# Depthwise convolution: TensorE's taps as three single-pass products, and another split of the taps

## The chip, the cores and the metric

The kernel runs on one core of a Trainium2 chip. The metric is the device time of one execution in microseconds (us). TensorE (PE) multiplies, VectorE (DVE), ScalarE (ACT) and GpSimd (POOL) work on tiles of 128 partitions, SyncE (SP) issues the loads; each engine works through its own list of instructions in order and waits on semaphores.

## The reference, cut to what matters

The whole program is eight sublayers over a sequence of 512 positions and 1024 channels: four mixers, each followed by a gated feed-forward layer. The change lies in the fourth mixer, a convolution module:

```
h = u @ w_pw1 + b_pw1
a, g = split(h, 2)                       # 1024 channels each
h = a * sigmoid(g)
y[s, ch] = sum over k in 0..30 of w[k, ch] * h[s - 30 + k, ch] + b[ch]
h = silu(layernorm(y))
out = h @ w_pw2 + b_pw2
```

The fourth line is the depthwise causal convolution: 31 taps for every channel, with zeros before the start of the sequence. All arrays are float32.

## The kernel before

Channels lie on partitions: 1024 channels are 8 chunks of 128, and a chunk's activations are one tile of 128 channels by 512 positions. Float32 matrix products elsewhere in the kernel are made from rounded parts: an operand becomes a high part (type fp32r, made by a ScalarE copy) and a low part (the operand less its high part), and TensorE adds three single-pass products, high by high, high by low and low by high. Lines 1298 to 1300 are such a group.

Weights come in slots of 256 columns. For every slot SyncE loads `w_raw`, ScalarE rounds it to `w_hi` (`round_half`, line 2031, two halves), GpSimd subtracts to `w_lo` (`low_part`, line 894, two halves), and TensorE multiplies. Both parts have two buffers, by the parity of the slot, so a slot is rounded only once the slot two before it is used. This stage has slots 0 to 7 (the first pointwise product; in the text they are numbered from the start of the stage) and 8 to 11 (the second).

The convolution of a chunk is shared by three engines. TensorE takes the first `PE_TAPS[c]` taps (`conv_taps`, line 1246): for a tap the stationary operand is a 128x128 diagonal with the tap's weight of each channel, the moving operand is `u_pad` from column k on, both plain float32, and the sum grows in a bank. ScalarE makes the diagonals (`diagonals`, line 2393) into two buffers, so those of chunk c wait until the taps of chunk c - 2 are done. GpSimd takes the last `POOL_TAPS[c]` taps (`pool_taps`, lines 909 to 916). VectorE takes the rest (`own_taps`, lines 2586 and 2588), and adds the sums of GpSimd (line 2591) and of TensorE (line 2593). Before the change:

```
PE_TAPS = [7, 7, 7, 7, 7, 9, 14, 15]
POOL_TAPS = [4, 4, 4, 4, 4, 4, 5, 5]
```

The order of work is written by hand on each engine:

- TensorE: slots 0 and 1; slot 2, taps 0; slot 3, taps 1; slot 4, taps 2; slot 5, taps 3, mean 0; slot 6, taps 4, mean 1; slot 7, taps 5, mean 2; taps 6, mean 3, taps 7, means 4 to 7. A mean (line 1255) adds a finished chunk over its channels. Then come the sums of squares (line 1277) and the second pointwise product. A slot waits for its banks, its low parts, and so on; the taps of a chunk wait for its gated input, its diagonals and its bank.
- VectorE: gate of chunks 0 and 1 (line 2598), own taps 0; gate of 2 and 3, own taps 1, own taps 2; gate of 4 and 5, own taps 3, own taps 4; gate of 6 and 7, own taps 5, 6 and 7.
- ScalarE: diagonals 0; rounding of slot 2; sigmoid of chunk 0 (line 2404), half of slot 3, sigmoid of chunk 1, other half of slot 3, diagonals 1 and 2; rounding of slot 4, sigmoids of 2 and 3 with the halves of slot 5, diagonals 3 and 4; slot 6, sigmoids of 4 and 5 with slot 7, diagonals 5 and 6; slot 8, sigmoids of 6 and 7 with slot 9, diagonals 7.
- GpSimd: low parts of slots 2 and 3, taps 0, low parts 4, taps 1, low parts 5, taps 2, low parts 6, taps 3, low parts 7, taps 4, low parts 8, taps 5, low parts 9, taps 6, taps 7, low parts 10.

The loop of ScalarE, whose order matters most:

```
for c in range(DC):
    if c % 2 == 0:
        round_slots(SLOT["cv"] + c, 1)
...
    round_half(SLOT["cv"] + 2 * (c // 2) + 1 + 2, c % 2)
    if c % 2 == 1:
        diagonals(c)
        if c + 1 < DC:
            diagonals(c + 1)
```

`round_slots(base, 1)` rounds both halves of slot base + 2.

Of the kernel before, what the change touches and what calls it, by code (L numbers as in the profile page):

```python
# [18 lines left out]
ALU = mybir.AluOpType  # L19
# [5 lines left out]
P = 128  # L25
# [14 lines left out]
HPG = MH // MG  # L40
NCONV = 24
TAPS = 31
PE_TAPS = [7, 7, 7, 7, 7, 9, 14, 15]
POOL_TAPS = [4, 4, 4, 4, 4, 4, 5, 5]
BIG = 1.0e30
SCORE_MASKED = -3.0e38
# [95 lines left out]
def build(nc, t, out, sublayers=8):  # L142

    with ExitStack() as ctx:
# [152 lines left out]
        ln_hi = in_big("ln_hi", [P, DC, S], 40, F32R)  # L297
        ln_lo = in_big("ln_lo", [P, DC, S], 56, F32R)
        tap_part = [in_big(f"tap_part{j}", [P, S], (17, 36)[j]) for j in range(2)]
        tap_diag = [in_big(f"tap_diag{j}", [P, 15, P], 72 + 7.5 * j) for j in range(2)]  # L300


        bank = [ctx.enter_context(nc.psum_tensor(f"bank{j}", [P, S], F32)) for j in range(8)]
# [67 lines left out]
        dve_chain = sem("dve_chain")  # L371
        y_squares = sem("y_squares")
        y_root = sem("y_root")
        sink_step = sem("sink_step")
        dt_step = sem("dt_step")
        dt_cm_in = sem("dt_cm_in")
        dt_turned = sem("dt_turned")
# [59 lines left out]
        diag_ready = sem("diag_ready")  # L437
        pe_taps_done = sem("pe_taps_done")
        taps_done = sem("taps_done")
        pool_taps_done = sem("pool_taps_done")  # L440
        own_tap_in = sem("own_tap_in")
        skip_done = sem("skip_done")
# [372 lines left out]
        def _(pool):  # L815
# [80 lines left out]

            taps_in = [0]

            def pool_taps(c):

                tap = lambda k: cols[:, ROWS["dw_w"] + DC * k + c:ROWS["dw_w"] + DC * k + c + 1]
                acc = sq[c % 2]
                k0 = TAPS - POOL_TAPS[c]
                pool.wait_ge(glu_done, c + 1)
                if c >= 1:
                    pool.wait_ge(pool_taps_done, c)
                if c >= 2:
                    pool.wait_ge(taps_done, c - 1)
                pool.tensor_scalar(acc[:], u_pad[:, c, k0:k0 + S], tap(k0), None, ALU.mult).then_inc(own_tap_in, 1)  # L909
                taps_in[0] += 1  # L910
                for k in range(k0 + 1, TAPS):
                    part = tap_part[k % 2]
                    pool.tensor_scalar(part[:], u_pad[:, c, k:k + S], tap(k), None, ALU.mult).then_inc(own_tap_in, 1)  # L913
                    taps_in[0] += 1
                    pool.wait_ge(own_tap_in, taps_in[0])
                    ins = pool.tensor_tensor(acc[:], acc[:], part[:], ALU.add)  # L916
                    if k < TAPS - 1:
                        ins.then_inc(own_tap_in, 1)
                        taps_in[0] += 1
                ins.then_inc(pool_taps_done, 1)  # L920
# [29 lines left out]
            while n < end_slot:  # L950
                if n == SLOT["out0"] + 2:
                    attention()
                if n == SLOT["odd"] + 6:
                    odd_units()
                    n = SLOT["out1"] + 2
                if n == SLOT["ssm"] + 3 + PROLOGUE // 2:
                    scan_pool(pool)
                    n = SLOT["ssm_out"] + 4
                if SLOT["cv"] + 4 <= n <= SLOT["cv"] + 10:
                    pool_taps(n - SLOT["cv"] - 4)  # L960
                if n == SLOT["cv"] + 10:
                    pool_taps(7)
                if n not in [SLOT[f"gu{f}"] for f in range(4)]:
                    low_part(n, n % 2, SLOT_K, widths.get(n, SLOT_W))

                    n += 1
                    continue
                with pool.Fori(0, FC // 2) as i:
                    for j in range(2):
                        low_part(i * 2 + (n + j), (n + j) % 2, SLOT_K, SLOT_W)  # L970
                n += N_GU
                with pool.Fori(0, 2) as i:
                    for j in range(6):
                        low_part(i * 6 + (n + j), (n + j) % 2, 8 if j % 3 < 2 else FC - 16, SLOT_W)
                n += N_DOWN
# [261 lines left out]
        def cv_pe(pe, take, freed, slot_cm, h_chunk, out_project, follows):  # L1237
            n0 = SLOT["cv"]

            def conv_taps(c):  # L1240

                pe.wait_ge(glu_done, c + 1)
                pe.wait_ge(diag_ready, c + 1)
                take(6 + c % 2, taps_done, c + 1)
                for k in range(PE_TAPS[c]):
                    ins = pe.matmul(bank[6 + c % 2][:], tap_diag[c % 2][:, k, :], u_pad[:, c, k:k + S],
                                    start=k == 0, stop=k == PE_TAPS[c] - 1)
                ins.then_inc(pe_taps_done, 1)

            def mean_part(c):  # L1250

                if c == 0:
                    take(4, centred, DC)
                pe.wait_ge(taps_done, c + 1)
                ins = pe.matmul(bank[4][:], ones[:], v_cm[:, c, :], start=c == 0, stop=c == DC - 1)  # L1255
                if c == DC - 1:
                    ins.then_inc(mean_summed, 1)

            for j in range(4):
                for q, by in enumerate((glu_done, sig_done)):  # L1260
                    dst = [take(2 * q + m, by, 2 * j + m + 1) for m in range(2)]
                    slot_cm(n0 + 2 * j + q, (n0 + 2 * j + q) % 2, lambda k: h_hi[:, k, :], lambda k: h_lo[:, k, :], dst,
                            before=h_chunk(6) if j == 0 and q == 0 else None)
                    if 2 * j + q >= 2:
                        conv_taps(2 * j + q - 2)
                    if 2 * j + q >= 5:
                        mean_part(2 * j + q - 5)
            conv_taps(6)
            mean_part(3)
            conv_taps(7)  # L1270
            for c in range(4, DC):
                mean_part(c)
            z0, r = SQ_BASE["ln"], ROOT_BASE["ln"]
            take(0, root_done, r + 1)
            for c in range(DC):
                pe.wait_ge(sq_ready, z0 + c + 1)
                pe.matmul(bank[0][:], ones[:], sq[(z0 + c) % 2][:], start=c == 0, stop=c == DC - 1).then_inc(sq_summed, 1)  # L1277
            out_project(SLOT["pw2"], 56, lambda k: ln_hi[:, k, :], lambda k: ln_lo[:, k, :],
                        before=lambda k: pe.wait_ge(h_ready, H_BASE["ln"] + k + 1), then_norm=follows(7))
# [723 lines left out]
        def _(act):  # L2003
# [382 lines left out]
            if n_sub > 6:  # L2386
                norm(6)
                def diagonals(c):
# [1 line left out]
                    if c >= 2:  # L2390
                        act.wait_ge(pe_taps_done, c - 1)
                    for k in range(PE_TAPS[c]):
                        ins = act.activation(tap_diag[c % 2][:, k, :], ident[:], ACT.Copy, scale=col("dw_w", DC * k + c))
                    ins.then_inc(diag_ready, 1)

                diagonals(0)
                for c in range(DC):

# [6 lines left out]
                                   ).then_inc(sig_done, 1)  # L2405
                    round_half(SLOT["cv"] + 2 * (c // 2) + 1 + 2, c % 2)
                    if c % 2 == 1:
                        diagonals(c)
                        if c + 1 < DC:
                            diagonals(c + 1)  # L2410
# [164 lines left out]
        def cv_dve(dve, link):  # L2575
            n0 = SLOT["cv"]
            pad = TAPS - 1
            link(dve.memset(u_pad[:, :, 0:pad], 0.0))

            def own_taps(c):  # L2580
                v = v_cm[:, c, :]
# [616 lines left out]
```

## Time and profile before

| | us |
|---|---|
| median of three runs | 2814.43 |
| lowest and highest run | 2808.67, 2814.97 |
| the profiled execution: time | 2813.69 |
| the profiled execution: span of its trace | 2811.8 |
| TensorE busy in the span | 2665.2 |
| VectorE, ScalarE, GpSimd busy in the span | 1126.8, 1069.8, 1302.6 |
| TensorE's taps (line 1246): busy, records | 64.0, 146 |
| VectorE's taps (line 2588): busy, instructions | 100.5, 133 |
| diagonals (line 2393): busy, instructions | 22.2, 73 |

The span is the time from the first to the last instruction of the trace; times inside the trace count from its start. The convolution stage lies between about 2200 and 2360. Every group of instructions has its line in the kernel, the number of instructions and the mean length of one; the idle time in square brackets is that of the engine before the instruction, with the instruction that ended it. Matmuls overlap, so their step is read from one start to the next. A float32 tap of the kernel before is one instruction in the kernel and two records in the trace.

### The profile page before, as it was taken

What the parts mean: (1) busy time and instruction counts of PE and PEld (TensorE: products, weight loads), DVE (VectorE), ACT (ScalarE), POOL (GpSimd) and SP (SyncE); (2) the same over time, 40 slices, a digit from 0 to 9 for tenths busy, and PEclk for the clock granted to TensorE, in tenths of its full rate; (3) what the DMA queues carried; (4) which work ended last, traced back from release to release, by engine and by line L of the source; (5) the groups of instructions that cost most, each with busy time, mean ns of one, the idle gap of its engine ahead of it and who ended that gap; (6) DMA issues with size and microseconds to landing.
All of it is one profiled execution on the core that took longest, in us unless ns stands there. A gap on an engine that the chain in (4) does not pass through costs nothing. (4 is left out here: it accounts for less than half of the span.)

```text
span 2811.8 us, 34699 instructions
## 1 busy us (share of the span) xinstructions
PE 2665.2 (95%) x13241; PEld 2134.3 (76%) x13241; DVE 1126.8 (40%) x1726; ACT 1069.8 (38%) x1718; POOL 1302.6 (46%) x747
## 2 busy tenths in 40 slices
PE   6997889999999899999999999999999997999998
PEld 5775558888877588888788887888888663888886
DVE  3168734222134342221237675233321497433312
ACT  3333544333236643332346555333322333433321
POOL 2322533444436534445356775444444485444441
PEclk8998889999999999999999999999999998999998
DMA  8654502323221013223221221232222210233221
GB/s 269 213 175 143 187 31 69 104 96 100 91 78 61 31 61 119 90 90 109 79 75 60 76 73 48 90 104 90 93 94 97 75 60 15 80 100 99 91 98 56
DMA packets 275967, 265.16 MB, mean 94 GB/s; under 512 B 20268, under 2 KB 274829, under 8 KB 275853
## 3 DMA queue, kind: packets, MB, share of 16 engines
q1 hardware_dynamic: 275853, 263.59, 29.5%
q8 instruction: 78, 1.28, 0.2%
q14 instruction: 36, 0.29, 0.0%
HBM read 261.47 MB, written 2.10 MB: 94 GB/s over the span
## 5 line engine op out<-in xcount | busy, mean ns | idle before, releaser
L894 POOL TENSOR_TENSOR w_lo<-w_raw,w_hi 128x1024 fp32r<-128x1024 f32 (+1 forms) x364 | 865.0, 2386 | 1272.5 <-ACT w_hi L2031 739.2
L1298 PE MATMUL bank<-h_hi,w_hi 128*128 128x512 f32 x1552 | 610.9, 394 | 16.0 <-DVE h_lo L2734 6.6
L1299 PE MATMUL bank<-h_lo,w_hi 128*128 128x512 f32 x1552 | 606.5, 391 | 0.0
L1300 PE MATMUL bank<-h_hi,w_lo 128*128 128x512 f32 x1552 | 606.3, 391 | 0.0
L2031 ACT ACTIVATE w_hi<-w_raw 128x1024 fp32r<-128x1024 f32 (+1 forms) x232 | 233.5, 1019 | 480.8 <-PE bank L1300 436.8
L1298 PEld LDWEIGHTS bank<-h_hi,w_hi 128*128 128x128 f32 x1552 | 293.2, 189 | 81.9 <-issue 16.4
L1299 PEld LDWEIGHTS bank<-h_lo,w_hi 128*128 128x128 f32 x1552 | 293.3, 189 | 62.4 <-issue 1.7
L1300 PEld LDWEIGHTS bank<-h_hi,w_lo 128*128 128x128 f32 x1552 | 293.0, 189 | 61.4
L1298 PE MATMUL bank<-a_hi,w_hi 128*128 128x512 f32 x704 | 273.9, 389 | 0.0
L1299 PE MATMUL bank<-a_lo,w_hi 128*128 128x512 f32 x704 | 273.9, 389 | 0.0
L1300 PE MATMUL bank<-a_hi,w_lo 128*128 128x512 f32 x704 | 273.9, 389 | 0.0
L2901 DVE TENSOR_TENSOR tmp<-sq,bank 128x512 f32<-128x512 f32 x88 | 60.5, 688 | 501.5 <-PE bank L1300 480.1
L2277 ACT ACTIVATE w_hi<-w_raw 128x1024 fp32r<-128x1024 f32 x176 | 182.9, 1053 | 170.1 <-PE bank L1300 167.8
L2905 DVE TENSOR_TENSOR a_lo<-tmp,a_hi 128x512 f32 x88 | 170.5, 1954 | 10.7 <-ACT a_hi L2292 10.5
L1299 PEld LDWEIGHTS bank<-a_lo,w_hi 128*128 128x128 f32 x704 | 132.2, 188 | 27.5
L1298 PEld LDWEIGHTS bank<-a_hi,w_hi 128*128 128x128 f32 x704 | 132.2, 188 | 27.5
L1300 PEld LDWEIGHTS bank<-a_hi,w_lo 128*128 128x128 f32 x704 | 132.2, 188 | 27.2
L753 POOL TENSOR_TENSOR w_lo<-w_raw,w_hi 128x1024 fp32r<-128x1024 f32 x38 | 92.3, 2434 | 96.5 <-ACT w_hi L2031 96.5
L2588 DVE SCALAR_TENSOR_TENSOR bank<-u_pad,cols,bank 128x512 f32<-128x512 f32 x125 | 94.5, 756 | 4.5
L2287 ACT ACTIVATE sq<-bank 128x512 f32<-128x512 f32 x44 | 26.3, 598 | 182.9 <-DVE tmp L2901 182.7
L2919 DVE TENSOR_TENSOR x_cm<-bank,x_cm 128x512 f32<-128x512 f32 x16 | 11.1, 692 | 197.6 <-PE bank L1300 197.6
L2921 DVE SCALAR_TENSOR_TENSOR x_cm<-bank,mod,x_cm 128x512 f32<-128x512 f32 x16 | 12.0, 751 | 195.2 <-PE bank L1300 195.2
(417 smaller groups left out, 4636.3 us busy)
## 6 DMA issues: line engine op xcount, KB each, us to landing
ada_w<-in_ada_w_dram SPq DMA_DIRECT2D x96, 512.0 KB, 6.0
w_raw<-in_ffn_gate_dram SPq DMA_DIRECT2D x22, 1024.0 KB, 5.3
w_raw<-in_ffn_up_dram SPq DMA_DIRECT2D x22, 1024.0 KB, 5.3
w_raw<-in_ffn_w_gate_dram SPq DMA_DIRECT2D x22, 1024.0 KB, 5.2
w_raw<-in_ffn_w_up_dram SPq DMA_DIRECT2D x22, 1024.0 KB, 5.2
w_raw<-in_ffn_down_dram SPq DMA_DIRECT2D x16, 1024.0 KB, 4.9
w_raw<-in_ssm_w_in_dram SPq DMA_DIRECT2D x16, 1024.0 KB, 5.2
w_raw<-in_ffn_w_down_dram SPq DMA_DIRECT2D x16, 1024.0 KB, 5.1
```

The costliest lines, as they stand in the source:

```text
L753: pool.tensor_tensor(w_lo[n % 2][:, :, half], w_raw[n % 2][:, :, half], w_hi[n % 2][:, :, half].bitcast(F32), ALU.subtract).then_inc(w_spl ...
L894: pool.tensor_tensor(w_lo[parity][:, 0:nk, half], w_raw[parity][:, 0:nk, half], w_hi[parity][:, 0:nk, half].bitcast(F32), ALU.subtract).th ...
L1298: pe.matmul(dst[m][:], hi, src_hi(k0 + k), start=first and k == 0, stop=False)
L1299: pe.matmul(dst[m][:], hi, src_lo(k0 + k), start=False, stop=False)
L1300: ins = pe.matmul(dst[m][:], lo, src_hi(k0 + k), start=False, stop=last and k == nk - 1)
L2031: act.activation(w_hi[n % 2][:, 0:nk, half], w_raw[n % 2][:, 0:nk, half], ACT.Copy).then_inc(w_rounded, 1)
L2277: act.activation(w_hi[par][:, :, half], w_raw[par][:, :, half], ACT.Copy).then_inc(w_rounded, 1)
L2287: act.activation(sq[q][:], bank[q][:], ACT.Silu).then_inc(silu_done, 1)
L2588: link(dve.scalar_tensor_tensor(out=acc[:] if k < k1 - 1 else v, in0=u_pad[:, c, k:k + S], scalar=tap(k), in1=acc[:], op0=ALU.mult, op1=AL ...
L2901: dve.tensor_tensor(tmp[q][:], sq[q][:], bank[2 + q][:], ALU.mult).then_inc(gated, 1)
L2905: dve.tensor_tensor(a_lo[:, bass.ds(i * 2 + q, 1), :], tmp[q][:].unsqueeze(1), hi, ALU.subtract).then_inc(a_ready, 1)
L2921: dve.scalar_tensor_tensor(out=x_cm[:, c, :], in0=bank[c % 4][:], scalar=mod[:, gate + c:gate + c + 1], in1=x_cm[:, c, :], op0=ALU.mult, o ...
```

## The change

TensorE's taps are made from parts as the other products are. Of the tap weights a rounded part `dw_hi` (ScalarE) and a low part `dw_lo` (VectorE) are made once, ahead of the stage. For every chunk ScalarE rounds the padded input to `u_hi` (`round_u`, 128x542), GpSimd subtracts it from the input to give `u_lo` (`split_u`, 128x542, ahead of the chunk's `pool_taps`), both in two buffers. ScalarE makes two diagonals for a tap, `diag_hi` and `diag_lo`, and TensorE three products. TensorE has 87 taps instead of 73, GpSimd the same 34, VectorE 127 instead of 141. Two semaphores carry the new order: `tap_split` (weights and rounded inputs) and `u_split` (low inputs); one unused semaphore goes.

```
-PE_TAPS = [7, 7, 7, 7, 7, 9, 14, 15]
+PE_TAPS = [9, 9, 9, 9, 9, 11, 15, 15]
...
+            def split_u(c):
+
+                pool.wait_ge(tap_split, 2 + c + 1)
+                pool.tensor_tensor(u_lo[c % 2][:], u_pad[:, c, :], u_hi[c % 2][:].bitcast(F32), ALU.subtract).then_inc(u_split, 1)
...
                 if SLOT["cv"] + 4 <= n <= SLOT["cv"] + 10:
+                    split_u(n - SLOT["cv"] - 4)
                     pool_taps(n - SLOT["cv"] - 4)
                 if n == SLOT["cv"] + 10:
+                    split_u(7)
                     pool_taps(7)
...
                 pe.wait_ge(diag_ready, c + 1)
+                pe.wait_ge(u_split, c + 1)
                 take(6 + c % 2, taps_done, c + 1)
                 for k in range(PE_TAPS[c]):
-                    ins = pe.matmul(bank[6 + c % 2][:], tap_diag[c % 2][:, k, :], u_pad[:, c, k:k + S],
-                                    start=k == 0, stop=k == PE_TAPS[c] - 1)
+                    hi, lo = diag_hi[c % 2][:, k, :], diag_lo[c % 2][:, k, :]
+                    pe.matmul(bank[6 + c % 2][:], hi, u_hi[c % 2][:, k:k + S], start=k == 0, stop=False)
+                    pe.matmul(bank[6 + c % 2][:], hi, u_lo[c % 2][:, k:k + S], start=False, stop=False)
+                    ins = pe.matmul(bank[6 + c % 2][:], lo, u_hi[c % 2][:, k:k + S], start=False, stop=k == PE_TAPS[c] - 1)
...
                     for k in range(PE_TAPS[c]):
-                        ins = act.activation(tap_diag[c % 2][:, k, :], ident[:], ACT.Copy, scale=col("dw_w", DC * k + c))
+                        at = DC * k + c
+                        act.activation(diag_hi[c % 2][:, k, :], ident[:], ACT.Copy, scale=col("dw_w", at))
+                        ins = act.activation(diag_lo[c % 2][:, k, :], ident[:], ACT.Copy, scale=dw_lo[:, at:at + 1])
                     ins.then_inc(diag_ready, 1)
 
+                def round_u(c):
+
+                    act.wait_ge(glu_done, c + 1)
+                    if c >= 2:
+                        act.wait_ge(pe_taps_done, c - 1)
+                    act.activation(u_hi[c % 2][:], u_pad[:, c, :], ACT.Copy).then_inc(tap_split, 1)
+
+                act.activation(dw_hi[:], col_range("dw_w", 0, TAPS * DC), ACT.Copy).then_inc(tap_split, 1)
+                act.wait_ge(tap_split, 2)
                 diagonals(0)
...
                     if c % 2 == 1:
+                        round_u(c - 1)
+                        round_u(c)
                         diagonals(c)
                         if c + 1 < DC:
                             diagonals(c + 1)
...
             link(dve.memset(u_pad[:, :, 0:pad], 0.0))
+            dve.wait_ge(tap_split, 1)
+            dve.tensor_tensor(dw_lo[:], col_range("dw_w", 0, TAPS * DC), dw_hi[:].bitcast(F32), ALU.subtract).then_inc(tap_split, 1)
```

## Rows read from the trace of the kernel before

**Rows 1.** Engines' busy time by stretch: PE, PEld, DVE, ACT, POOL, PEclk, DMA share, GB/s.

```profile
2210.00:2220.00 10.00, 8.39 (x37) 6.67 (x36) 3.14 (x5) 4.85 (x10) 5.08 (x3) 1.00 0.34 106
2220.00:2352.80 132.80, 132.79 (x442) 82.76 (x441) 116.81 (x155) 35.38 (x81) 112.78 (x71) 1.00 0.17 56
2352.80:2358.40 5.60, 0.00 (x0) 0.00 (x0) 4.87 (x7) 0.00 (x0) 3.98 (x3) 0.93 0.00 0
```

**Rows 2.** Chain of waits at the stage's end: start, length, what ran.

```profile
2355.61 1.27 POOL sq L916
2356.97 0.70 DVE v_cm L2591
...
2358.44 2.09 PE bank L1255 x2
```

**Rows 3.** Timeline of GpSimd in the stage: start, length, engine, line, operation.

```profile
2238.75 4.77 POOL L894 TENSOR_TENSOR w_lo<-w_raw,w_hi 128x1024 fp32r<-128x1024 f32 x2 [7.57 <-ACT w_hi L2031]
...
2309.39 4.77 POOL L894 TENSOR_TENSOR w_lo<-w_raw,w_hi 128x1024 fp32r<-128x1024 f32 x2 [6.33 <-ACT w_hi L2031]
...
2324.76 4.69 POOL L894 TENSOR_TENSOR w_lo<-w_raw,w_hi 128x1024 fp32r<-128x1024 f32 x2
2329.41 1.59 POOL L909 TENSOR_SCALAR sq<-u_pad,cols 128x512 f32<-128x512 f32 x1
...
2343.27 1.56 POOL L909 TENSOR_SCALAR sq<-u_pad,cols 128x512 f32<-128x512 f32 x1 [0.16 <-issue]
```

**Rows 4.** Timeline of ScalarE: the diagonals of chunk 6.

```profile
2304.15 4.21 ACT L2393 ACTIVATE tap_diag<-ident,cols 128x128 f32<-128x128 f32 x14 [15.05 <-PE bank L1246]
```

**Rows 5.** Timeline of VectorE: a long wait, one chunk's taps, the last tap.

```profile
2241.78 0.75 DVE L2598 SCALAR_TENSOR_TENSOR u_pad<-bank,cols,tmp 128x512 f32<-128x512 f32 x1 [5.45 <-ACT tmp L2404]
...
2285.33 14.21 DVE L2588 SCALAR_TENSOR_TENSOR bank<-u_pad,cols,bank 128x512 f32<-128x512 f32 x18
...
2355.68 0.75 DVE L2588 SCALAR_TENSOR_TENSOR v_cm<-u_pad,cols,bank 128x512 f32<-128x512 f32 x1
```

**Rows 6.** Timeline of TensorE in the stage and behind it.

```profile
2246.30 4.03 PE L1246 MATMUL bank<-u_pad,tap_diag 128*128 128x512 f32 x9
...
2262.10 0.39 PE L1299 MATMUL bank<-h_lo,w_hi 128*128 128x512 f32 x1
...
2263.00 0.39 PE L1300 MATMUL bank<-h_hi,w_lo 128*128 128x512 f32 x1
...
2280.15 6.17 PE L1246 MATMUL bank<-u_pad,tap_diag 128*128 128x512 f32 x14
2286.15 1.02 PE L1255 MATMUL bank<-v_cm,ones 128*128 128x512 f32 x2
...
2303.95 1.02 PE L1255 MATMUL bank<-v_cm,ones 128*128 128x512 f32 x2
...
2315.71 6.60 PE L1246 MATMUL bank<-u_pad,tap_diag 128*128 128x512 f32 x15
...
2350.05 2.74 PE L1255 MATMUL bank<-v_cm,ones 128*128 128x512 f32 x6
2358.44 2.08 PE L1255 MATMUL bank<-v_cm,ones 128*128 128x512 f32 x2 [5.65 <-DVE v_cm L2593]
2362.05 10.33 PE L1277 MATMUL bank<-sq,ones 128*128 128x512 f32 x16 [1.54 <-ACT sq L2416]
2379.67 0.76 PE L1298 MATMUL bank<-ln_hi,w_hi 128*128 128x512 f32 x1 [7.29 <-DVE ln_lo L3168]
...
2384.91 0.40 PE L1298 MATMUL bank<-ln_hi,w_hi 128*128 128x512 f32 x1
```

**Rows 7.** Groups by line, 2190 to 2400: busy time, mean ns of one.

```profile
L894 POOL TENSOR_TENSOR w_lo<-w_raw,w_hi 128x1024 fp32r<-128x1024 f32 x20 | 47.9, 2413 | 76.8 <-ACT w_hi L2031 76.8
...
L2423 ACT ACTIVATE ln_hi<-sq 128x512 fp32r<-128x512 f32 x4 | 2.5, 632 | 0.1
```

**Rows 8.** One tile's instructions, `tap_part`: shortest, median and longest in ns.

```profile
L916 POOL TENSOR_TENSOR sq<-sq,tap_part x26: 1259/1270/1819, 2224.1 to 2355.6; 128x512 f32<-128x512 f32 x26
```

More of the change, by code:

```diff
@@ L299, in build @@
         tap_part = [in_big(f"tap_part{j}", [P, S], (17, 36)[j]) for j in range(2)]
-        tap_diag = [in_big(f"tap_diag{j}", [P, 15, P], 72 + 7.5 * j) for j in range(2)]
+        diag_hi = [in_big(f"diag_hi{j}", [P, 15, P], 72 + 7.5 * j, F32R) for j in range(2)]
+        diag_lo = [in_big(f"diag_lo{j}", [P, 15, P], 40 + 7.5 * j, F32R) for j in range(2)]
+        u_hi = [in_big(f"u_hi{j}", [P, TAPS - 1 + S], 56 + 2.5 * j, F32R) for j in range(2)]
+        u_lo = [in_big(f"u_lo{j}", [P, TAPS - 1 + S], 61 + 2.5 * j, F32R) for j in range(2)]
+        dw_hi = in_big("dw_hi", [P, TAPS * DC], 66, F32R)
+        dw_lo = in_big("dw_lo", [P, TAPS * DC], 67, F32)
         bank = [ctx.enter_context(nc.psum_tensor(f"bank{j}", [P, S], F32)) for j in range(8)]
@@ L373, in build @@
         y_root = sem("y_root")
-        sink_step = sem("sink_step")
         dt_step = sem("dt_step")
@@ L439, in build @@
         taps_done = sem("taps_done")
+        u_split = sem("u_split")
+        tap_split = sem("tap_split")
         pool_taps_done = sem("pool_taps_done")
```

## The prediction

> **What bounds the kernel now.** I read first the busy time by stretch, then the chain of waits backwards from the end, then the timeline of each engine in the convolution stage, last the groups by line. Nothing outside this stage changes, so the whole answer is by how much its end moves.
>
> In the stage TensorE is busy for 132.79 of the 132.80 us from 2220 to 2352.8, its granted clock at the high level throughout [rows 1], and one would take it for the bound. Its own order ends earlier, though: it stands idle for the 5.6 us before 2358.4 [rows 1]. The chain of waits names who is last: GpSimd's last tap sum for channel chunk 7 (start 2355.61, 1.27 us), then VectorE's two adds, then TensorE's mean of chunk 7 at 2358.44 [rows 2]. From there to the pointwise product everything hangs in series on that mean.
>
> GpSimd's list is followed back in its timeline [rows 3]. It runs from 2309.39 to 2356.87 without a wait on another engine: low parts of weight slot 8, taps of chunk 5, low parts of slot 9, taps of chunks 6 and 7. What started it at 2309.39 is ScalarE's rounding of slot 8, which stands behind the diagonals of chunk 6 (2304.15, 14 of them, 4.21 us), and these waited 15.05 us for TensorE's taps of chunk 4 [rows 4], which ended at 2303.95 [rows 6]. So the end of the stage is: taps of chunk 4 on TensorE, one set of diagonals on ScalarE, then 47.5 us of GpSimd.
>
> VectorE is second by a hair: its last own tap ends at 2356.43 [rows 5], 0.44 us before GpSimd. Its long waits lie early: 5.45 us at 2241.78, for ScalarE's sigmoid of chunk 2 [rows 5].
>
> **The change, part by part.** I number chunks 0 to 7 and the weight slots of this stage 0 to 9.
>
> *TensorE's taps.* A tap of before is two records; chunk 3's 14 take from 2280.15 to 2286.15, so 0.857 us a tap. Single-pass products follow each other at 0.225 us (2262.10 to 2263.00, four steps), three make 0.68 us [rows 6]. The shifted start of the moving operand does not slow the old taps, so I add nothing for it. Chunks 0 to 4 go from 7 x 0.857 = 6.0 to 9 x 0.68 = 6.1 us (+0.12), chunk 5 from 7.7 to 7.5, chunk 6 from 12.0 to 10.2, chunk 7 from 12.9 to 10.2. Over all chunks 73 x 0.857 = 62.6 become 87 x 0.68 = 59.2 us. These 3.4 us lie in chunks 5 to 7, behind waits that grow (below), and give nothing.
>
> *VectorE's taps.* An own tap costs 14.21 / 18 = 0.79 us [rows 5]. Chunk 0's two lie before the wait of 5.45 us and give nothing; chunks 1 to 5 lose two each, chunk 6 one: 11 x 0.79 = 8.7 us off VectorE's list. They would count only if VectorE set the end.
>
> *GpSimd's splits.* Eight subtractions of 128x542 are added, one ahead of each chunk's taps. The nearest rows are GpSimd's two-input operations, 128x512 at 1.27 us and 128x1024 at 2.41 us [rows 7, 8]; in between, 542 columns give 1.34 us. Bounds: 1.26 and 1.82 us, the fastest and slowest 128x512 [rows 8]. Nothing is taken off GpSimd: its tap counts stay.
>
> *ScalarE.* Each tap now needs two diagonals, at 4.21 / 14 = 0.30 us apiece, 0.294 from one to the next [rows 4]. Chunk 2 goes from 7 to 18 (+11 x 0.294 = 3.2 us), chunk 4 the same, chunk 6 from 14 to 30 (+16 x 0.294 = 4.7 us). These three sets stand ahead of the rounding of slots 4, 6 and 8. The odd chunks' sets stand ahead of nothing that is late: ScalarE waits for TensorE behind them. The roundings of u cost 0.63 us each at 512 columns [rows 7]. Their wait on TensorE's earlier taps is the one the diagonals behind them had already, and their wait on the gate is over by then, so they only push the odd sets. The one-time split of the tap weights sits at 2199, while GpSimd idles and the next rounding is not due before 2205: nothing.
>
> *The new waits.* TensorE's taps of a chunk now wait for GpSimd's split, and behind them stands the next slot. GpSimd's split waits for ScalarE's rounding of u, and behind it stand its taps and the next low parts. Walked through:
>
> Chunk 0: split done near 2222, taps not due before 2229; end +0.12. Then the 18 diagonals of chunk 2: GpSimd's low parts of slot 4, at 2238.75 before [rows 3], start at 2238.75 + 0.12 + 3.2 = 2242.1, take 4.77, and the split of chunk 1 ends at 2248.2. TensorE wants it at 2246.30 + 0.12 [rows 6]: it waits 1.8 us. Chunk 2's split is not waited for. At chunk 3 the pattern of chunk 1 repeats (18 diagonals, two low parts, split): another 1.8 us. With 5 x 0.12 the taps of chunk 4 end 4.1 us later, at 2308.1.
>
> Then the last chain: +4.7 us for chunk 6's diagonals puts GpSimd's start at 2309.39 + 8.8 = 2318.2, and the splits of chunks 5, 6 and 7 add 3 x 1.34 = 4.0. GpSimd ends at 2356.87 + 12.8 = 2369.7. VectorE, now early, waits for it at chunks 6 and 7.
>
> In the same walk TensorE wants chunk 5 at 2315.71 [rows 6] + 4.1 = 2319.8 and gets it at 2318.2 + 4.77 + 1.34 = 2324.3, 4.5 us late. Adding GpSimd's pieces of [rows 3] (10.6 for chunk 5's taps, as slot 8 and they fill 2309.39 to 2324.76; 4.65 for slot 9; 13.9 for chunk 6's) and a split each, it gets chunk 6 at 2340.9 after 8.2 us idle and chunk 7 at 2356.1 after 4.1 us idle; that one is done at 2366.3, and three means end at 2368.9. So TensorE is not last, and waits only 2.3 us before the last mean.
>
> That shortens the tail. After its 5.65 us of idling the last mean's two records took 2.08 us, while the three means at 2350.05 took 2.74 together, 0.9 each [rows 6]. In the stretch 2210 to 2220, TensorE idle for 1.6 of 10 us, the granted clock stayed at the high level [rows 1]; 2.3 us is nearer to that than to 5.65. I take 2.08 - 0.9 = 1.2 us off. The sums of squares after it, 10.33 us [rows 6], I leave: TensorE has little to do for some 5 us around the mean, as in 2352.8 to 2358.4. At the high clock 8 x 0.86 us would be their floor, 3.3 us less: the other bound.
>
> **Sum:** 4.1 + 4.7 + 4.0 - 1.2 = +11.6 us. The profiled execution took 2813.69 us (span 2811.8), 0.74 below the median of the three runs. Forecast: 2813.69 + 11.6 = 2825.3 us, 0.4% slower. With splits at 1.26 or 1.82 us (five count) it is 11.2 or 14.0, so its own range is 2824 to 2829.
>
> **The clock.** The stalls of 4.1 to 8.2 us are as long as gaps after which the granted clock had fallen (5.65 and 7.29 us); after the second the products came at half their rate for 5.2 us, from 2379.67 to 2384.91 [rows 6]. One cold start thus costs 2.6 us: chunk 6 would end at 2353.7 and its mean at 2354.6, before the split of 2356.1 and so hidden; chunk 7's three means end at 2371.5, 0.3 us after VectorE's last add, which I leave out. The Trainium skill (TensorE: Matmul & The Clock Gate, Part 1: The HAM clock gate) has the low clock as the default, which only sustained activity lifts and idling brings back, and so speaks against a change that puts holes into TensorE's stream. By that rule, with which these rows agree, the sum is 11.9 instead of 11.6.
>
> **Rivals.**
>
> *VectorE sets the end (faster).* If GpSimd's longer list were covered, the 8.7 us would count: 2805. For it: VectorE ended only 0.44 us before GpSimd. Against: GpSimd's 47.5 us have no gap and lose nothing. It decides only if GpSimd's taps of chunk 7 ended before 2348, so 9 us earlier than now, while three splits join them. 9%.
>
> *The tail stays at the high clock.* Means and sums of squares save 1.2 + 3.3 us: 12.8 - 4.5 = +8.3, 2822.0. For it: TensorE is busy to 2369. Against: the low activity around the mean. 15%.
>
> *The taps are no cheaper.* If a product with a shifted start takes long enough that a tap stays at 0.857 us, chunks 0 to 4 grow by 5 x 9 x 0.18 = 8 us, all in the chain: 2833. Against: the old shifted reads run like the unshifted ones. 7%.
>
> *The clock stays low to the end.* Chunks 6 and 7 at half the clock take 20.4 us each: from 2340.9 to 2361.3, mean 1.7, taps to 2383.4, four means to 2390.3 instead of 2360.5: up to +30, 2844. 7%.
>
> **The numbers.** Forecast 62%. No change within 0.3% (8.4 us, about what a measurement tells apart) is the warm tail: 15%. Faster by more: 9%. Slower by more: forecast and the two slow rivals, 76%. The range 2817 to 2834 leaves out the faster case and the low clock, 16%.
>
> **What would show it.** GpSimd's low parts of slot 8 start near 2318; its last tap ends near 2370; VectorE idles before its adds of chunks 6 (about 9 us) and 7; TensorE waits some 1.8 us before the taps of chunks 1 and 3, and 4 to 8 us before those of 5, 6 and 7; products of taps at 0.225 us. It is wrong if the splits run well under 1.3 us, if ScalarE makes a diagonal in under 0.2 us, or if GpSimd reaches slot 8's low parts before 2312.

## The result, and the profile after

The changed kernel takes 2821.96 us (median of 12 runs, 2817.75 to 2827.57); the kernel before, timed beside it, takes 2812.03 (12 runs, 2808.67 to 2814.97). The ratio is 1.0038, interval 1.0029 to 1.0046: 0.4% slower, 9.9 us by the medians. The forecast was 2825.3 us, 0.4% slower, range 2817 to 2834. Two executions of this study, one of the rebalanced kernel (4687 us) and one of the kernel before beside it (4982 us), ran at a far lower granted clock and are left out of every median and ratio.

The profiled execution took 2818.38 us (span 2816.4), 4.7 more than that of before. Its stage begins earlier in the trace, though. VectorE's first gated input, the mark from which I count below, in the timeline of VectorE of the kernel before:

```profile
2212.14 0.75 DVE L2598 SCALAR_TENSOR_TENSOR u_pad<-bank,cols,tmp 128x512 f32<-128x512 f32 x1 [11.92 <-ACT tmp L2404]
```

And the timeline of VectorE after: the same mark, its waits for GpSimd at the adds of chunks 6 and 7, and its last addition to the residual.

```profile
2205.50 0.75 DVE L2629 SCALAR_TENSOR_TENSOR u_pad<-bank,cols,tmp 128x512 f32<-128x512 f32 x1 [10.75 <-ACT tmp L2431]
...
2350.41 1.55 DVE L2622 TENSOR_TENSOR v_cm<-sq,v_cm 128x512 f32<-128x512 f32 x1 [7.46 <-POOL sq L927]
...
2365.14 0.69 DVE L2622 TENSOR_TENSOR v_cm<-sq,v_cm 128x512 f32<-128x512 f32 x1 [3.83 <-POOL sq L927]
...
2429.70 0.75 DVE L2905 SCALAR_TENSOR_TENSOR x_cm<-bank,cols,x_cm 128x512 f32<-128x512 f32 x1 [4.07 <-PE bank L1316]
```

The first gate comes at 2212.14 before and 2205.50 after; in the profiles of the experiments it lies anywhere from 2203.2 to 2212.8, with the same work ahead of it. So one compares from this gate. To the last mean it is 146.3 us before (2358.44, [rows 6]) and 161.1 after (2366.61, below), 14.8 more; to the first product behind the layer norm 167.5 and 178.7; and to VectorE's last addition to the residual after the second pointwise product (last line above; 2425.96 in the trace of before) 213.8 and 224.2, 10.4 more. That is close to the 9.9 of the medians.

The busy time by stretch, after, over the stage and its last microseconds (columns as in [rows 1]):

```profile
2220.00:2360.80 140.80, 127.48 (x514) 101.11 (x513) 108.62 (x138) 60.28 (x162) 116.58 (x74) 0.94 0.14 45
2360.80:2366.60 5.80, 4.17 (x13) 2.07 (x11) 1.90 (x3) 0.00 (x0) 4.10 (x3) 1.00 0.00 0
```

TensorE, which had no hole in the stage before, now has 13.3 us of them, and its granted clock there fell from 1.00 to 0.94. Yet it works nearly to the end: 4.17 of the last 5.8 us, at the high level, where it was idle before. The chain of waits at the stage's end:

```profile
2350.30 1.11 POOL u_lo L908
2351.41 1.98 POOL sq L920
...
2363.77 1.27 POOL sq L927
...
2365.14 0.70 DVE v_cm L2622
...
2365.87 0.70 DVE v_cm L2624
...
2366.61 1.14 PE bank L1271 x2
```

The same three engines in the same order as [rows 2], with the new subtraction (line 908) in GpSimd's list. GpSimd's timeline after: the low parts of weight slot 4, then those of slot 8 and the list behind them.

```profile
2235.69 4.75 POOL L900 TENSOR_TENSOR w_lo<-w_raw,w_hi 128x1024 fp32r<-128x1024 f32 x2 [9.71 <-ACT w_hi L2047]
...
2314.61 4.71 POOL L900 TENSOR_TENSOR w_lo<-w_raw,w_hi 128x1024 fp32r<-128x1024 f32 x2 [9.22 <-ACT w_hi L2047]
2319.28 1.15 POOL L908 TENSOR_TENSOR u_lo<-u_pad,u_hi 128x542 fp32r<-128x542 f32 x1
...
2335.76 1.33 POOL L908 TENSOR_TENSOR u_lo<-u_pad,u_hi 128x542 fp32r<-128x542 f32 x1
...
2350.26 1.15 POOL L908 TENSOR_TENSOR u_lo<-u_pad,u_hi 128x542 fp32r<-128x542 f32 x1
...
2363.77 1.26 POOL L927 TENSOR_TENSOR sq<-sq,tap_part 128x512 f32<-128x512 f32 x1
```

No wait stands between 2314.61 and 2365.03, as none stood before; what changed is when the list starts and how long it is. The start is set by ScalarE, whose timeline after shows the first diagonal of chunk 6, the last of 30, and the rounding of slot 8:

```profile
2304.69 0.40 ACT L2410 ACTIVATE diag_hi<-ident,cols 128x128 fp32r<-128x128 f32 x1 [10.90 <-PE bank L1263]
...
2313.19 0.40 ACT L2411 ACTIVATE diag_lo<-ident,dw_lo 128x128 fp32r<-128x128 f32 x1
2313.48 2.00 ACT L2047 ACTIVATE w_hi<-w_raw 128x1024 fp32r<-128x1024 f32 x2
```

8.79 us from the first diagonal to the rounding, 0.293 a diagonal. And TensorE's timeline after: the waits of the taps (chunks 1, 3, 5, 6), chunk 7's first tap, and the tail.

```profile
2241.80 0.47 PE L1261 MATMUL bank<-u_hi,diag_hi 128*128 128x512 f32 x1 [1.64 <-DVE u_pad L2629]
...
2278.55 0.77 PE L1261 MATMUL bank<-u_hi,diag_hi 128*128 128x512 f32 x1 [2.10 <-POOL u_lo L908]
2279.11 0.63 PE L1262 MATMUL bank<-u_lo,diag_hi 128*128 128x512 f32 x1
2279.54 0.63 PE L1263 MATMUL bank<-u_hi,diag_lo 128*128 128x512 f32 x1
...
2282.03 0.40 PE L1263 MATMUL bank<-u_hi,diag_lo 128*128 128x512 f32 x1
...
2286.43 1.02 PE L1271 MATMUL bank<-v_cm,ones 128*128 128x512 f32 x2
...
2320.68 0.77 PE L1261 MATMUL bank<-u_hi,diag_hi 128*128 128x512 f32 x1 [4.27 <-POOL u_lo L908]
...
2337.35 0.77 PE L1261 MATMUL bank<-u_hi,diag_hi 128*128 128x512 f32 x1 [5.31 <-POOL u_lo L908]
...
2350.64 1.02 PE L1271 MATMUL bank<-v_cm,ones 128*128 128x512 f32 x2
2351.66 0.47 PE L1261 MATMUL bank<-u_hi,diag_hi 128*128 128x512 f32 x1
...
2366.61 1.12 PE L1271 MATMUL bank<-v_cm,ones 128*128 128x512 f32 x2 [1.64 <-DVE v_cm L2624]
2369.28 7.67 PE L1293 MATMUL bank<-sq,ones 128*128 128x512 f32 x16 [1.54 <-ACT sq L2445]
2384.23 0.77 PE L1314 MATMUL bank<-ln_hi,w_hi 128*128 128x512 f32 x1 [7.28 <-DVE ln_lo L3199]
...
2387.77 0.40 PE L1316 MATMUL bank<-ln_hi,w_lo 128*128 128x512 f32 x1
```

The profile puts the wait at 2241.80 down to a gated input of VectorE's. What chunk 1 waited for is GpSimd's split behind the low parts of 2235.69: it ended at 2241.54, 0.26 us before the tap, as the splits of chunks 3 and 5 end 0.26 and 0.25 us before theirs. After the wait of 2.10 us the products of chunk 3 step by 0.43 us (the first by 0.56) up to 2282.03, then by 0.23: TensorE's low clock level (1.2 GHz) and its high one (2.4).

### The profile page after: what moved, and what is told of

Its sections match the earlier page's. It is cut to its first block and busy times, and to the rows that moved or that the text cites. A ratio compares the mean times of both kernels' runs of the same rounds, so it can differ in the third digit from the quotient of the medians.

```text
span 2816.4 us, 35041 instructions
## 1 busy us (share of the span) xinstructions
PE 2663.3 (95%) x13353; PEld 2155.3 (77%) x13353; DVE 1122.4 (40%) x1714; ACT 1103.3 (39%) x1826; POOL 1313.5 (47%) x755
## 5 line engine op out<-in xcount | busy, mean ns | idle before, releaser
L2619 DVE SCALAR_TENSOR_TENSOR bank<-u_pad,cols,bank 128x512 f32<-128x512 f32 x112 | 84.7, 756 | 4.0
```

The source lines that it names most:

```text
L2619: link(dve.scalar_tensor_tensor(out=acc[:] if k < k1 - 1 else v, in0=u_pad[:, c, k:k + S], scalar=tap(k), in1=acc[:], op0=ALU.mult, op1=AL ...
```

## The experiments

The theory is that of the prediction: the end of the stage is a chain of queues. TensorE's taps of chunk 4 release ScalarE's diagonals of chunk 6, behind which stands the rounding of slot 8, behind which stands GpSimd's whole remaining list. The doubled diagonals and the splits lengthen this chain; TensorE's own work does not set the end. The rivals are that TensorE is the bound now (by its products, or by the clock that its holes cost), and that what was lost is the tap counts' doing and not the queues'.

All are told by one table. The time is the median; "from the gate" counts in the profile from VectorE's first gated input to the last mean, and to the last addition to the residual; "before" is the median of the kernel before on the same chip. The two columns from the gate are read from one execution each; their differences from the kernel before agree with those of the medians within 3.5 us.

| | us | before | ratio (interval) | gate to mean | gate to addition |
|---|---|---|---|---|---|
| before | 2812.03 | | | 146.3 | 213.8 |
| after | 2821.96 | 2812.03 | 1.0038 (1.0029 to 1.0046) | 161.1 | 224.2 |
| e1_late_diag | 2805.79 | 2810.17 | 0.9983 (0.9974 to 0.9992) | 141.1 | 207.0 |
| e2_before_late_diag | 2810.12 | 2810.17 | 1.0005 (0.9995 to 1.0015) | 148.0 | 214.0 |
| e3_no_split | 2813.78 | 2810.17 | 1.0013 (1.0004 to 1.0022) | 152.2 | 217.6 |
| e4_one_diag | 2813.00 | 2810.17 | 1.0013 (1.0003 to 1.0022) | 151.3 | 214.5 |
| e5_late_2_4 | 2816.05 | 2811.01 | 1.0023 (1.0009 to 1.0038) | 155.2 | 220.3 |
| e6_late_6 | 2813.83 | 2811.01 | 1.0019 (1.0005 to 1.0033) | 152.1 | 217.1 |
| e7_old_taps | 2811.25 | 2811.01 | 1.0007 (0.9994 to 1.0019) | 149.3 | 214.0 |
| e8_new_taps_fp32 | 2816.49 | 2811.01 | 1.0022 (1.0009 to 1.0036) | 154.2 | 220.2 |
| e9_rebalanced | 2801.73 | 2812.12 | 0.9966 (0.9954 to 0.9978) | 139.8 | 206.5 |
| e10_low_parts_last | 2815.67 | 2812.12 | 1.0010 (1.0000 to 1.0020) | 148.9 | 214.3 |

**The order of ScalarE alone.** The changed kernel, with the diagonals of chunks 2, 4 and 6 moved behind the rounding of slots 4, 6 and 8:

```
                     if c % 2 == 0:
                         round_slots(SLOT["cv"] + c, 1)
+                        if c >= 2:
+                            diagonals(c)
...
                         diagonals(c)
-                        if c + 1 < DC:
-                            diagonals(c + 1)
```

> The changed kernel, with one reordering on ScalarE: the diagonals of the even chunks 2, 4 and 6 are made after the rounding of weight slots 4, 6 and 8 instead of before it. Nothing is added or left out. Theory (GpSimd's list sets the end of the stage, and it starts late because the doubled diagonals stand ahead of the rounding that releases it): GpSimd's low parts of slots 4, 6 and 8 start right behind its taps, TensorE's waits before the taps of chunks 1 and 3 and 5 to 7 go (at most 0.5 us each), GpSimd is done some 18 us earlier, and VectorE's shorter tap list now sets the end: first gate to last mean about 142 us instead of 161.1 (before the change: 146.3), time about 5 us below the kernel before the change. Rival (TensorE's taps are what costs, by cold clock or slower products): the waits go, but the stage is no shorter than 152 us and the time stays above the kernel before. Second rival (GpSimd's splits alone are the cost, wherever the list starts): about 157 us, 5 us slower than before.

Measured: 141.1 us to the mean, 20 less than after, and 5 less than before; the time falls below that of the kernel before. GpSimd's list in this kernel, low parts of slots 4 and 8:

```profile
2231.72 5.20 POOL L900 TENSOR_TENSOR w_lo<-w_raw,w_hi 128x1024 fp32r<-128x1024 f32 x2
...
2298.03 4.77 POOL L900 TENSOR_TENSOR w_lo<-w_raw,w_hi 128x1024 fp32r<-128x1024 f32 x2
...
2348.93 1.26 POOL L927 TENSOR_TENSOR sq<-sq,tap_part 128x512 f32<-128x512 f32 x1
```

The brackets are gone: neither is waited for. Counted from its gate (2211.31), slot 8 starts at 86.7 us, where it was 97.2 before and 109.1 after. The tail in TensorE's timeline:

```profile
2336.84 0.47 PE L1261 MATMUL bank<-u_hi,diag_hi 128*128 128x512 f32 x1 [0.50 <-POOL u_lo L908]
...
2347.42 2.74 PE L1271 MATMUL bank<-v_cm,ones 128*128 128x512 f32 x6
2352.45 1.74 PE L1271 MATMUL bank<-v_cm,ones 128*128 128x512 f32 x2 [2.29 <-DVE v_cm L2624]
```

Of all the waits of the taps 0.50 us is left, with every product, split and diagonal of the change still there. VectorE ends its own taps at 2350.95, 0.76 us after GpSimd. TensorE is not the bound.

**The same order in the kernel before.** The same edit, made to the kernel before the change:

> The kernel before the change, with the same reordering on ScalarE (diagonals of chunks 2, 4 and 6 after the rounding of slots 4, 6 and 8). Nothing is added or left out. Theory: GpSimd ends some 8 us earlier (its idle time before slot 8's low parts goes), but VectorE's tap list, which ended 0.44 us before GpSimd, then sets the end alone: first gate to last mean 145.5 to 146.3 us, no change in time within 1 us. Rival (GpSimd alone bounds the stage): up to 6 us shorter. With this the gain of the first run is told apart: if this one gains nothing, that gain belongs to the change, freed of its queueing, and not to the reordering as such.

No change of time. The mean is 1.7 us later than before, outside the expectation: GpSimd is released early here too, but VectorE, with its 141 taps, ends the stage. The last tap sum in GpSimd's timeline and the last own tap in VectorE's:

```profile
2346.61 1.27 POOL L916 TENSOR_TENSOR sq<-sq,tap_part 128x512 f32<-128x512 f32 x1
...
2353.70 0.75 DVE L2588 SCALAR_TENSOR_TENSOR v_cm<-u_pad,cols,bank 128x512 f32<-128x512 f32 x1
```

From the gate of chunk 3 to this tap VectorE waits for nothing, in this kernel and in the kernel before. It ends the tap 2.2 us later here (146.5 us from the gate, 144.3 before), and its six adds of GpSimd's sums in this stretch take 7.9 us instead of 5.6: GpSimd, released earlier, now works on two-input operations beside other adds (last section). So the gain of the first experiment is not the order's own. With the order free, the change is worth 148.0 - 141.1 = 6.9 us of the stage. VectorE's own taps end 6.9 us earlier with it (139.6 against 146.5 us from the gate), which goes with its shorter list, priced by the prediction at 8.7.

**No splits.** The changed kernel without GpSimd's subtractions:

```
-                    split_u(n - SLOT["cv"] - 4)
...
-                    split_u(7)
...
-                pe.wait_ge(u_split, c + 1)
+                pe.wait_ge(tap_split, 2 + c + 1)
...
-                    pe.matmul(bank[6 + c % 2][:], hi, u_lo[c % 2][:, k:k + S], start=False, stop=False)
+                    pe.matmul(bank[6 + c % 2][:], hi, u_hi[c % 2][:, k:k + S], start=False, stop=False)
```

> The changed kernel without GpSimd's eight subtractions; TensorE's second product of each tap reads the high part of the input instead of the low part, and TensorE waits for ScalarE's rounding of the input instead. Three products a tap stay, and all diagonals. It leaves out the low part of the input. Theory: five splits lie in the chain (two by the waits of chunks 1 and 3, three in GpSimd's last list), so first gate to last mean is shorter than the changed kernel's 161.1 us by 5 x 1.2 = 6 us, and by up to 1.6 us more if the clock no longer falls at chunk 3: 153 to 155.5 us. Rival (the diagonals alone are the cost): 160 us or more.

8.9 us of the 14.8 come back, 0.8 more than the expected range allows: the waits before chunks 1 and 3 go whole (1.64 and 2.10 us) and not by the length of a split each. TensorE does as many products as before this edit and waits for GpSimd nowhere until its last mean (TensorE's timeline):

```profile
2364.94 2.08 PE L1269 MATMUL bank<-v_cm,ones 128*128 128x512 f32 x2 [12.64 <-DVE v_cm L2622]
```

It stands idle for 12.64 us there, and the stage is still 5.9 us longer than before. Slot 8's low parts start 103.4 us from the gate, 6.1 later than before: 4.7 of that is the price of chunk 6's diagonals, which are still there.

**Half the diagonals.** The changed kernel with one diagonal for a tap:

```
-                    hi, lo = diag_hi[c % 2][:, k, :], diag_lo[c % 2][:, k, :]
+                    hi = lo = diag_hi[c % 2][:, k, :]
...
-                        act.activation(diag_hi[c % 2][:, k, :], ident[:], ACT.Copy, scale=col("dw_w", at))
-                        ins = act.activation(diag_lo[c % 2][:, k, :], ident[:], ACT.Copy, scale=dw_lo[:, at:at + 1])
+                        ins = act.activation(diag_hi[c % 2][:, k, :], ident[:], ACT.Copy, scale=col("dw_w", at))
```

> The changed kernel with one diagonal a tap instead of two: ScalarE makes only the high diagonal, and TensorE's third product reads it again. Three products a tap stay, and all of GpSimd's splits. It leaves out the low part of the tap weights. Theory: the sets ahead of the rounding of slots 4, 6 and 8 shrink by 9, 9 and 15 times 0.293 us (2.6, 2.6, 4.4), which takes the waits before chunks 1 and 3 away and starts GpSimd's last list some 8 us earlier: first gate to last mean 151 to 153 us instead of 161.1. Rival (the splits alone are the cost): 160 us or more.

9.8 us come back, within the expectation: 15 x 0.293 = 4.4 at chunk 6, and the waits of 1.64 and 2.10 us before chunks 1 and 3 go, with the low clock behind the second (1.6, below).

**Diagonals 2 and 4 late, or 6 late.** The edit of the first experiment for some chunks alone: `if c in (2, 4)` in one kernel, `if c in (6,)` in the other.

> The changed kernel with the late order on ScalarE for chunks 2 and 4 alone: their diagonals come after the rounding of slots 4 and 6; chunk 6's stay ahead of slot 8. Nothing is left out. Theory: TensorE's waits before the taps of chunks 1 and 3 (1.64 and 2.10 us in the changed kernel) go, and with them the 1.6 us that chunk 3's taps lost at the low clock behind the second wait; GpSimd's last list still starts late. First gate to last mean 154.5 to 156.5 us (161.1 in the changed kernel, 146.3 before the change). If the low clock at chunk 3 has nothing to do with that wait: 157 to 158. Rival (everything hangs on chunk 6's diagonals): 160 us or more.

> The changed kernel with the late order on ScalarE for chunk 6 alone: its diagonals come after the rounding of slot 8; those of chunks 2 and 4 stay ahead of slots 4 and 6. Nothing is left out. Theory: GpSimd's 9.2 us of idling before slot 8's low parts go, TensorE's waits at chunks 1 and 3 stay: first gate to last mean 151.5 to 153.5 us. Rival (the waits at chunks 1 and 3 carry most of the loss): 157 us or more.

5.9 us come back from the first and 9.0 from the second, both within the expectation. The first undoes the waits that make chunk 4's taps late; the second takes the 30 diagonals (8.8 us) out of the chain. Together they are 14.9 of the first experiment's 20; the rest comes only with both. (With 6 late the last means are merged into one row; the mean is placed at the end of VectorE's last add, 2360.4.) In the kernel with 2 and 4 late, the low parts of slot 8 in GpSimd's timeline show the step that remains:

```profile
2306.49 4.71 POOL L900 TENSOR_TENSOR w_lo<-w_raw,w_hi 128x1024 fp32r<-128x1024 f32 x2 [16.55 <-ACT w_hi L2047]
```

GpSimd comes there earlier and waits longer for the rounding, 16.55 us instead of 9.22; slot 8 starts 103.3 us from the gate, 16.6 later than with all three sets late.

**Taps or products.** The three products with the tap counts of before (7, 7, 7, 7, 7, 9, 14, 15), and the plain float32 taps of before with the new counts:

```
-PE_TAPS = [9, 9, 9, 9, 9, 11, 15, 15]
+PE_TAPS = [7, 7, 7, 7, 7, 9, 14, 15]
```

> The changed kernel with the tap counts of before on TensorE (7, 7, 7, 7, 7, 9, 14, 15, so 73) and so 14 taps more on VectorE: the products in parts alone, without the new split of the taps. Nothing is left out. Theory: every set of diagonals is double that of before (14, 14, 28), the splits are there, but TensorE's taps are shorter (4.8 us a chunk): the sum in the chain is about +3 us, first gate to last mean 148.5 to 151 us, time within 0.3% of the kernel before. Rival (the splits and double diagonals cost the same whatever the counts): 157 us or more.

> The kernel before the change with the new tap counts (9, 9, 9, 9, 9, 11, 15, 15) in plain float32: the new split of the taps alone. Nothing is left out. Theory: ten taps more by the end of chunk 4 lengthen TensorE's part of the chain by 10 x 0.857 = 8.6 us, chunk 6's diagonals by 0.3, so GpSimd starts 9 us later: first gate to last mean 154 to 156 us, time 7 to 9 us above the kernel before. Rival (VectorE's shorter list pays for it): 146 us or less.

To the mean the products alone cost 3.0 us and the counts alone 7.9, both within the expectation. For the second the time is 5.5 us more by the medians, below the expected 7 to 9, which its interval (2.5 to 10) does not exclude; to the last addition it is 6.4, since the last mean, after a wait of 2.44 us, took 1.21 us instead of 2.08. Neither half gains anything in this order, and the halves do not add: on top of the products the new counts cost 11.8 us (149.3 to 161.1). So the rival of the tap counts has a share: most of the 14.8 us come with the counts, though through the same queues. With the old counts TensorE waits 0.52 and 0.49 us before chunks 1 and 3, with the new ones 1.64 and 2.10, and two taps more are 1.4 us for each chunk up to chunk 4.

**Low parts of slots 8 and 9 last, and a rebalanced split.** GpSimd makes these low parts, which the second pointwise product wants, behind its last taps:

```
-                    low_part(n, n % 2, SLOT_K, widths.get(n, SLOT_W))
+                    if n == SLOT["cv"] + 10:
+                        for held in (n - 2, n - 1):
+                            low_part(held, held % 2, SLOT_K, widths.get(held, SLOT_W))
+                    if n not in (SLOT["cv"] + 8, SLOT["cv"] + 9):
+                        low_part(n, n % 2, SLOT_K, widths.get(n, SLOT_W))
```

The one kernel has this alone; the other has it with the late diagonals and with

```
+PE_TAPS = [7, 8, 8, 9, 9, 13, 15, 15]
+POOL_TAPS = [4, 4, 5, 5, 4, 5, 4, 6]
```

> The changed kernel with one edit on GpSimd: the low parts of slots 8 and 9 are made behind the taps of chunk 7 instead of ahead of the taps of chunks 5 and 6. ScalarE's order and all counts stay. Nothing is left out. Theory: GpSimd's last list no longer waits for the rounding that stands behind chunk 6's 30 diagonals, and is 9.5 us shorter, so VectorE and TensorE, held by the gates of chunks 6 and 7, end the stage: first gate to last mean 147 to 150 us instead of 161.1, although all diagonals, splits and waits at chunks 1 and 3 are still there. Rival (the diagonals or TensorE's stalls hold the end whatever stands in GpSimd's list): 155 us or more.

> The changed kernel with three edits: the late order of the first run on ScalarE; GpSimd makes the low parts of slots 8 and 9, which TensorE reads only after the layer norm, behind its last taps instead of ahead of the taps of chunks 5 and 6; and the taps shared anew, TensorE 7, 8, 8, 9, 9, 13, 15, 15, GpSimd 4, 4, 5, 5, 4, 5, 4, 6. Nothing is left out. Theory (three lists that end together, and 9.5 us of GpSimd's in the way): first gate to last mean 136 to 139.5 us, against 146.3 before the change and 141.2 with the late order alone; time 7 to 10 us below the kernel before. Rival (VectorE and GpSimd slow each other, or TensorE is the bound already): 141 us or more, no better than the late order alone.

The first: 12.2 us come back, and VectorE ends the stage, its last own tap (VectorE's timeline) behind GpSimd's last tap sum (GpSimd's):

```profile
2352.36 1.27 POOL L927 TENSOR_TENSOR sq<-sq,tap_part 128x512 f32<-128x512 f32 x1
...
2356.53 0.75 DVE L2623 SCALAR_TENSOR_TENSOR v_cm<-u_pad,cols,bank 128x512 f32<-128x512 f32 x1
```

The second is the fastest kernel of the study, 0.34% below the kernel before (10.4 us by the medians) and 0.7% below the change. Its mean comes at 139.8, just outside the expectation, and its interval, from another chip, meets that of the late diagonals alone, so the rebalancing on top is not shown to pay. Where its last microseconds went, in GpSimd's timeline:

```profile
2348.61 9.72 POOL L900 TENSOR_TENSOR w_lo<-w_raw,w_hi 128x1024 fp32r<-128x1024 f32 x4
```

and in VectorE's:

```profile
2348.76 2.74 DVE L2626 TENSOR_TENSOR v_cm<-sq,v_cm 128x512 f32<-128x512 f32 x1 [1.92 <-POOL sq L927]
2351.53 0.69 DVE L2628 TENSOR_TENSOR v_cm<-bank,v_cm 128x512 f32<-128x512 f32 x1
```

The low parts, now without a use before the end, start just as VectorE makes its last add from two tiles; the add takes 2.74 us instead of the 0.69 of the changed kernel's add of chunk 7.

## Why the prediction was right

The chain held step by step; its terms did not all hold in size, and that their sum came so close owes something to luck. One count ahead of it is wrong: the new `PE_TAPS` add up to 86 and not 87, which leaves VectorE 128 taps and not 127. No term rests on it (86 x 0.68 is 58.5 us instead of 59.2, in a saving that was put at nothing). The terms, counted from the gate:

| term | forecast | measured | from |
|---|---|---|---|
| taps of chunk 4 end later | 4.1 | 7.2 | ScalarE's first diagonal of chunk 6: 92.0 before ([rows 4]), 99.2 after |
| chunk 6's diagonals, 30 for 14 | 4.7 | 4.7 | from there to slot 8's low parts: 5.24 before ([rows 3]), 9.92 after |
| splits of chunks 5, 6, 7 | 4.0 | 2.9 | from there to GpSimd's end: 47.5 before, 50.4 after |
| last mean to the layer norm's first product | -1.2 | -3.6 | 21.2 before ([rows 6]), 17.6 after |
| behind it | 0 | -0.8 | 46.3 and 45.5 to the addition |
| sum | 11.6 | 10.4 | |

*The waits before chunks 1 and 3* (4.1 against 7.2) is the term that was most mis-sized. The waits were forecast at 1.8 each and are 1.64 and 2.10. What the forecast left out is that behind the second of them TensorE falls to its low clock: chunk 3's taps take 7.88 us (2278.55 to 2286.43) instead of the 6.1 reckoned. Its paragraph on the clock weighed only the gaps of 4.1 us and more. Also, a tap product steps by 0.233 us and not by 0.225: the 27 products of chunks 0, 2 and 4 take 6.29 us each. Of the 3.1 us that the term lacks, 1.6 are the low clock and 1.0 the longer step over five chunks; the rest lies in the waits. The two other kernels that keep this wait (diagonals 6 late, low parts last) lose the same stretch.

*The diagonals* were right to the tenth: the count times the row's step.

*The splits* were put at 1.34 us by interpolation between 512 and 1024 columns. The tile's line over all eight, shortest, median and longest in ns:

```profile
L908 POOL TENSOR_TENSOR u_lo<-u_pad,u_hi x8: 1135/1242/1819, 2214.3 to 2350.3; 128x542 fp32r<-128x542 f32 x8
```

The three that count took 1.15, 1.33 and 1.15. The rest of the difference is in the taps between them, which ran a little shorter. "The splits run well under 1.3 us" had been named as what would make the forecast wrong; of the 1.1 us missing here, 0.4 are the splits'.

*The tail.* The last mean took 1.12 us after a wait of 1.64 (2.08 before): 1.0 less, where 1.2 was forecast. The sums of squares, which were left at 10.33, took 7.67, at the high clock (granted clock 1.00 from 2366.61 to 2377): most of the other bound of 3.3 us came true. The low activity around the mean, for which the forecast left them slow, did not bring the clock down. The layer norm's products, too, ran low for 3.5 us (2384.23 to 2387.77) instead of 5.2 ([rows 6]), the 0.8 of the last term. So the rival of the warm tail had much of its mechanism right (3.6 us of its 4.5), and its 2822.0 us is the time measured. Had the first term not been 3.1 us larger than forecast and rival both had it, the change would have stayed under the 0.3% that the prediction called no change. The two errors nearly cancel in the sum: that is the luck.

*The waits later on.* Before chunk 5: 4.27 us (forecast 4.5). Before chunk 6: 5.31; the forecast was 8.2, less the 2.6 us of a cold start of chunk 5, which did happen (0.77, 0.63 us products). Before chunk 7 none, where about 4 were forecast: the split ended at 2351.41, 0.25 us before TensorE was done with chunk 6 and mean 3 (2351.66). All of it was hidden, as reckoned. VectorE idled 7.46 us at chunk 6 (forecast about 9) and 3.83 at chunk 7.

*The rivals.* VectorE does set the end once GpSimd's list is released early (late diagonals: its last own tap and adds run to 2352.4, GpSimd ended at 2350.2), and then the change gains, as that rival said (4.4 us by the medians, not its 8.7); the condition it needed was not met in the change itself. The taps are cheaper: 0.70 us against 0.857. The clock did not stay low to the end: chunk 7's products start at 0.47 us and stay at the high level.

## What to carry to other kernels

Where engines work through lists in a fixed order, the cost of added work is read from what stands behind it in its own list: 16 small copies on a ScalarE that idled 15 us made the chain to the stage's end 4.7 us longer, since the rounding that starts GpSimd's last 47 us stood behind them. Before an operation is doubled on an engine with time to spare, look whether something urgent can be put ahead of it: here that move alone turned a loss of 9.9 us into a gain of 4.4. And a change that relieves an engine (VectorE's 8.7 us) gives nothing until the one that ends last is relieved too; try the two together before giving either up.

## What the runs showed of the hardware that was not expected

**A wait's length alone does not tell whether the clock falls.** The wait of 2.1 us before chunk 3 cost about eight products at the low level in all three kernels that have it (the changed kernel, diagonals 6 late, low parts last), and not always at once. In the kernel with the low parts last the first product is still at the high level and the fall comes behind it (TensorE's timeline):

```profile
2283.71 0.47 PE L1265 MATMUL bank<-u_hi,diag_hi 128*128 128x512 f32 x1 [2.10 <-POOL u_lo L908]
2284.01 0.57 PE L1266 MATMUL bank<-u_lo,diag_hi 128*128 128x512 f32 x1
2284.38 0.63 PE L1267 MATMUL bank<-u_hi,diag_lo 128*128 128x512 f32 x1
```

In the kernel with diagonals 6 late a longer wait left the clock high, and a shorter one brought it down three products later:

```profile
2331.13 0.47 PE L1261 MATMUL bank<-u_hi,diag_hi 128*128 128x512 f32 x1 [3.25 <-POOL u_lo L908]
2331.44 0.39 PE L1262 MATMUL bank<-u_lo,diag_hi 128*128 128x512 f32 x1
...
2345.54 0.47 PE L1261 MATMUL bank<-u_hi,diag_hi 128*128 128x512 f32 x1 [2.81 <-POOL u_lo L908]
...
2346.62 0.63 PE L1262 MATMUL bank<-u_lo,diag_hi 128*128 128x512 f32 x1
```

Before a chunk's taps in these runs, waits of 1.58 to 1.66 us left it high each time, and those of 3.74 us and more (4.27 and 5.31 in the changed kernel, 4.26 and 5.78 with diagonals 2 and 4 late, 3.74 and 7.29 with the old counts, 7.80 with one diagonal) brought it down each time; in between, the outcome has to be bounded from both sides. The Trainium skill (TensorE: Matmul & The Clock Gate, Part 1: The HAM clock gate) says of the start of a kernel that the number of slow products differs between runs of one and the same kernel. No run here shows that for the start, and behind the wait of 2.1 us the number hardly differs. What does differ is the moment of the fall: up to this wait the three kernels have the same instructions, and it comes at the first product in two of them and at the second in the third.

**An add on VectorE slows beside GpSimd.** VectorE's add of two tiles of 128x512 takes 0.69 us by itself and 2.74 when it starts 0.15 us after one of GpSimd's two-input operations of 128x1024, as shown above; at 2272.04 and 2331.11 of the changed kernel, where such an operation begins or runs as well, it takes 2.90 and 2.48. The Trainium skill (SBUF — State Buffer, Who interferes with whom) says that a VectorE instruction with two SBUF inputs contends with a GpSimd instruction that reads SBUF, that the shared ports are locked and not shared out, and that the order of issue decides who is blocked. The rows agree: a half of the low parts takes 2.41 us ([rows 7]), so the one begun at 2348.61 would end at 2351.0, and the add that began behind it ended at 2351.5. They agree on the order too: in the kernel before, VectorE's add at 2346.38 came 0.07 us ahead of a tap sum of GpSimd's and took its 0.69 us, while the tap sum took 1.75 us instead of the usual 1.27 ([rows 8]).
